# Seven-product form for four step pairs of a gate or feed-forward panel, a six-slot ring in the feed-forward block too, and two more gate panels a layer

## What is computed

```python
h = rms_norm(x, norm_g)
u = h @ w_in                      # 2048 -> 15944 columns, 8192 of them gates
...
for n, (y, z) in enumerate(((y_a, a_z), (y_b, b_z), (y_c, c_z), (y_m, m_z))):
    branch = y.reshape(B, S, W).astype(dt) * jax.nn.silu(z)
    merged = merged + jax.nn.sigmoid(gate_all[:, :, n]) * (branch @ w_branch[n])
return x + merged @ w_out
```

```python
gt, up = jnp.split(rms_norm_2(x, g_ffn) @ w_gate_up, 2, axis=-1)
return x + (jax.nn.silu(gt) * up) @ w_down
```

## Time and profile before

| | |
|---|---|
| median of the runs | 3272.08 us |
| the profiled execution's own time | 3272.8 us |
| its span, first to last instruction | 3271.0 us |
| PE busy | 3258.1 us |
| DVE busy | 2203.4 us |
| ACT busy | 1638.9 us |
| POOL (GpSimd) busy | 321.3 us |
| read from HBM | 609.80 MB, 189 GB/s over the span |

### The profile page before, as it was taken

The page is one execution under the profiler, slowest core; times in us unless marked ns, Lnnn a source line. Parts: engine busy times, 40 slices in busy tenths (PEclk is TensorE's granted clock), DMA queues, the critical chain, the costliest instruction groups (busy, mean ns, idle before and its releaser), DMA issues.

```text
span 3271.0 us, 39924 instructions
## 1 busy us (share of the span) xinstructions
PE 3258.1 (100%) x15091; PEld 2699.7 (83%) x15091; DVE 2203.4 (67%) x2476; ACT 1638.9 (50%) x2085; POOL 321.3 (10%) x282
## 2 busy tenths in 40 slices
PE   8999999999999999999999999999999999999999
PEld 7888888888888888888888888888888888888887
DVE  5466655588865656555888655575555578888887
ACT  6444445455544444454555445455444455555554
POOL 0111241100000102411000011160000100000000
PEclk9999999999999999999999999999999999999999
DMA  8665565666666655556665675554565656556655
GB/s 300 191 185 166 165 177 162 188 206 193 217 193 205 182 167 166 173 164 186 202 211 183 208 226 170 172 179 144 193 192 183 186 187 204 187 194 204 194 193 180
DMA packets 303808, 619.77 MB, mean 189 GB/s; under 512 B 24961, under 2 KB 29441, under 8 KB 302465
## 3 DMA queue, kind: packets, MB, share of 16 engines
q1 hardware_dynamic: 303616, 617.22, 60.9%
HBM read 609.80 MB, written 7.34 MB: 189 GB/s over the span
## 4 chain that ended last, share of the span: by engine, by line
PE 100%; DMA 0%; DVE 0%; ACT 0%; SPq 0%; issue 0%
PE G L1127 69%; PE X L1048 6%; PE X L1046 6%; PE X L1047 6%; PE X L826 2%; PE G L1048 2%; PE G L1047 2%; PE G L1046 2%; PE X L942 1%; PE X L914 1%; PE G L1121 1%; PE X L969 0%; PE X L968 0%; PE X L935 0%; PE X L916 0%; PE X L889 0%
## 5 line engine op out<-in xcount | busy, mean ns | idle before, releaser
L1452 DVE TENSOR_TENSOR w_lo<-raw,w_hi 128x1024 fp32r<-128x1024 f32 (+1 forms) x1016 | 1236.9, 1223 | 942.2 <-ACT w_hi L1148 915.4
L1148 ACT ACTIVATE w_hi<-raw 128x1024 fp32r<-128x1024 f32 (+1 forms) x1016 | 1052.8, 1041 | 1265.3 <-PE G L1127 1129.0
L1127 PE MATMUL G<-w_hi,xh 128*128 128x512 f32 x1984 | 796.0, 401 | 0.0
L1127 PE MATMUL G<-w_hi,xl 128*128 128x512 f32 x1984 | 775.0, 391 | 0.0
L1127 PE MATMUL G<-w_lo,xh 128*128 128x512 f32 x1984 | 772.7, 389 | 0.0
L1127 PE MATMUL G<-w_hi,yh 128*128 128x512 f32 x1256 | 499.3, 398 | 8.5 <-DVE w_lo L1452 8.5
L1127 PE MATMUL G<-w_hi,yl 128*128 128x512 f32 x1256 | 491.2, 391 | 0.0
L1127 PE MATMUL G<-w_lo,yh 128*128 128x512 f32 x1256 | 490.0, 390 | 0.0
L1127 PEld LDWEIGHTS G<-w_hi,xl 128*128 128x128 f32 x1984 | 372.3, 188 | 81.0
L1127 PEld LDWEIGHTS G<-w_hi,xh 128*128 128x128 f32 x1984 | 372.9, 188 | 73.9 <-issue 2.7
L1127 PEld LDWEIGHTS G<-w_lo,xh 128*128 128x128 f32 x1984 | 373.3, 188 | 72.2
(11 more groups left out here) (261 smaller groups left out, 3164.3 us busy)
## 6 DMA issues: line engine op xcount, KB each, us to landing
raw<-in_w_in SPq DMA_DIRECT2D x572, 512.0 KB, 3.6
raw<-in_w_gate_up SPq DMA_DIRECT2D x176, 512.0 KB, 4.1
raw<-in_w_down SPq DMA_DIRECT2D x88, 512.0 KB, 4.5
raw<-in_w_out SPq DMA_DIRECT2D x64, 512.0 KB, 4.2
raw_more<-in_w_in SPq DMA_DIRECT2D x52, 512.0 KB, 4.4
raw<-in_w_branch SPq DMA_DIRECT2D x48, 512.0 KB, 3.8
raw<-in_w_mem_kv SPq DMA_DIRECT2D x32, 512.0 KB, 6.3
raw<-in_w_o SPq DMA_DIRECT2D x32, 512.0 KB, 3.6
```

The lines of the kernel that those rows point to most:

```text
L1127: mm = M.matmul(G[blk.g][:, t, :], a[:, blk.kk + k, tok], ringed(w, blk, c)[:, j, :], start=(k == 0 and q == 0), stop=(k == blk.kt - 1 and ...
L1148: A(high_of(c)[:, 0:size_of(c)], source_of(c), ACT.Copy).then_inc(hi_done, 1)
L1452: V.tensor_tensor(low_of(c)[:, 0:n], source_of(c), high_of(c)[:, 0:n].bitcast(F32), ALU.subtract).then_inc(lo_done, 1)
```

## The change

Four edits, all in tables:

- `SEVENS` replaces `SEVEN`: the steps 1, 2, 4 and 5 take the seven-product form instead of 1, 3 and 5. One panel a layer, branch b's second, is `LIGHT` and keeps three (1, 2, 4).
- The gate blocks 0 and 1 of branch c become a panel, so a layer has six.
- `wide` now holds for every panel, and for the `down` blocks from the second group on: they use six slots. The first such use in the feed-forward block waits for the end of the last attention heads.
- The heads of m and b come four units apart instead of five: m from r+120, b from r+140; the forms, now four, at r+145, 149, 153, 157. The first panel begins at r+162. In the feed-forward block the fourth form is hung 18 units behind the first.

```diff
-SEVEN = (1, 3, 5)
+SEVENS = {0: (1, 2, 4, 5), 1: (1, 2, 4, 5), FF: (1, 2, 4, 5)}
+LIGHT = {("panel", l, "b", 1): (1, 2, 4) for l in range(DEPTH)}
+FORMS = max(len(s) for s in SEVENS.values())
...
+        self.seven = LIGHT.get(name, SEVENS[name[1]]) if kind == "panel" else ()
...
-                if br in WIDE_BRANCHES and (br, n // 2) != ("c", 0):
+                if br in WIDE_BRANCHES:
...
-        b.wide = (b.kind == "panel" and b.name[1] != FF) or (b.name[0] == "merge" and b.name[1] < DEPTH and ("panel", *b.name[1:3], b.name[3] // 2) in panels)
+        b.wide = b.kind == "panel" or (b.name[0] == "down" and b.name[1] > 0) or (b.name[0] == "merge" and b.name[1] < DEPTH and ("panel", *b.name[1:3], b.name[3] // 2) in panels)
...
-            soft(r + 121 + 5 * h, "m", l, h)
+            soft(r + 120 + 4 * h, "m", l, h)
         for h in range(H):
-            c = r + 146 + 5 * h
+            c = r + 140 + 4 * h
             at(c, "b_turn", l, h)
...
-        for i in range(len(SEVEN)):
-            at(r + 150 + 6 * i, "forms", l, i)
+        for i in range(len(SEVENS[l])):
+            at(r + 145 + 4 * i, "forms", l, i)
...
-    for i in range(len(SEVEN)):
+    for i in range(len(SEVENS[FF])):
         at(end_of("up", 0) + 4 + 6 * i, "forms", FF, i)
...
-                for l in range(DEPTH):
+                for l in PANEL_EVENTS:
                     if c in EXT_FIRST[l]:
-                        act.wait_ge(y_ready, Y_OF["norm", "b", l, H - 1] + 1)
-                        act.wait_ge(o_squared, NORM_OF["norm", "b", l, H - 1] + 1)
+                        if l == FF:
+                            act.wait_ge(y_ready, Y_OF["s_pv", "l", 2, HEADS2 - 1] + 1)
+                            act.wait_ge(x_sq_done, 16)
+                        else:
+                            act.wait_ge(y_ready, Y_OF["norm", "b", l, H - 1] + 1)
+                            act.wait_ge(o_squared, NORM_OF["norm", "b", l, H - 1] + 1)
```

More of the change, by code:

```diff
@@ L68, in chunks @@
     def chunks(self):
-        return sum(4 if s in SEVEN else 2 for s in range(STEPS)) if self.kind == "panel" else self.kt // self.ck
+        return sum(4 if s in self.seven else 2 for s in range(STEPS)) if self.kind == "panel" else self.kt // self.ck
     @property
@@ L162, in in_units @@
             loads += [(b, 2 * s), (b, 2 * s + 1)]
-            if s in SEVEN:
+            if s in blk.seven:
                 units += [(b, "low", s, k0 + 1), (b, "first", s, k0), (b, "sums13", s, None), (b, "sums24", s, None)]
@@ L179 @@
 LAST_PANEL = {l: max(b for b in PANELS if BLOCKS[b].name[1] == l) for l in PANEL_EVENTS}
-FORMS_DONE = {l: len(SEVEN) * (i + 1) for i, l in enumerate(PANEL_EVENTS)}
+FORMS_DONE = {l: sum(len(SEVENS[m]) for m in PANEL_EVENTS[:i + 1]) for i, l in enumerate(PANEL_EVENTS)}
 FF_PANEL = {b: i for i, b in enumerate(b for b in PANELS if BLOCKS[b].name[1] == FF)}
-STEM_ENDS = {SUMS_UNIT[b, SEVEN[-1]]: b for b in PANELS}
+STEM_END = {b: SUMS_UNIT[b, BLOCKS[b].seven[-1]] for b in PANELS}
+STEM_ENDS = {c: b for b, c in STEM_END.items()}
 def in_slots(wide, width):
@@ L212 @@
 BEHIND = {c: range(max(R_BEHIND[c], 0), R_BEHIND[c + 1]) for c in range(N_CHUNKS)}
-EXT_FIRST = {l: [min(c for c in range(FIRST_WIDE[l], N_CHUNKS) if U_SLOT[c] == k) for k in (4, 5)] for l in range(DEPTH)}
-EXT_LOAD = {l: min(r for r, (b, _s) in enumerate(LOADS) if b >= FIRST_PANEL[l] and R_SLOT[r] >= RING) for l in range(DEPTH)}
+EXT_FIRST = {l: [min(c for c in range(FIRST_WIDE[l], N_CHUNKS) if U_SLOT[c] == k) for k in (4, 5)] for l in PANEL_EVENTS}
+EXT_LOAD = {l: min(r for r, (b, _s) in enumerate(LOADS) if b >= FIRST_PANEL[l] and R_SLOT[r] >= RING) for l in PANEL_EVENTS}
 BLOCK = {b.name: i for i, b in enumerate(BLOCKS)}
@@ L552, in hybrid_program @@
         sums = over("sums", "arena", 0, [P, 2, 4, NB], F32)
-        form_hi_in = over("form_hi_in", "arena", 8192, [P, len(SEVEN), 4, P], F32R)
-        form_hi_ff = over("form_hi_ff", "arena", 4096, [P, len(SEVEN), 4, P], F32R)
+        form_hi_in = over("form_hi_in", "arena", 8192, [P, FORMS, 4, P], F32R)
+        form_hi_ff = over("form_hi_ff", "arena", 4096, [P, FORMS, 4, P], F32R)
         form_hi = {0: form_hi_in, 1: form_hi_in, FF: form_hi_ff}
-        form_lo = over("form_lo", "tmp", 0, [P, len(SEVEN), 4, P], F32R)
+        form_lo = over("form_lo", "tmp", 0, [P, FORMS, 4, P], F32R)
         form = [tmp[:, 3072 + 512 * i:3584 + 512 * i].rearrange("p (f t) -> p f t", t=P) for i in range(2)]
@@ L743, in back @@
             def back(l):
-                sp.wait_ge(lo_done, SUMS_UNIT[LAST_PANEL[l], SEVEN[-1]] + 1)
+                sp.wait_ge(lo_done, STEM_END[LAST_PANEL[l]] + 1)
                 if l:
@@ L1053, in by_form @@
             def by_form(l, s, f):
-                i = SEVEN.index(s)
+                i = SEVENS[l].index(s)
                 return form_hi[l][:, i, f, :], form_lo[:, i, f, :]
@@ L1073, in panel @@
                     _b, what, s, _r = UNITS[c]
-                    first, last = s == SEVEN[0], s == SEVEN[-1]
+                    first, last = s == blk.seven[0], s == blk.seven[-1]
                     pe.wait_ge(lo_done, c + 1)
@@ L1151, in stem @@
                 _, l, br, m = BLOCKS[b].name
-                act.wait_ge(mm_done, SUMS_UNIT[b, SEVEN[-1]] + 1)
+                act.wait_ge(mm_done, STEM_END[b] + 1)
                 if b == FIRST_PANEL[l]:
@@ L1852, in x_forms @@
             def x_forms(l, i):
-                k, n = 2 * SEVEN[i], FORM_N["forms", l, i]
+                k, n = 2 * SEVENS[l][i], FORM_N["forms", l, i]
                 if n >= 2:
@@ L1907, in _ @@
                 for i in range(H):
-                    if i < len(SEVEN):
+                    if i < len(SEVENS[l]):
                         x_forms(l, i)
```

## The result

The kernel takes 3286.87 us (median, 3286.63 to 3286.96) beside 3272.05 us for the kernel before on the same chip: a ratio of 1.0044, 95% interval [1.0033, 1.0056]. It is **slower by 14.8 us**; the forecast was 3261.8 us, and its range ended at 3269. None of the rivals describes what happened. (The title counts two more gate panels a layer; it is one more, made of two gate blocks, so six where there were five. And it leaves out the edit that decided the result, the heads four units apart.)

A forecast was written before the change was run, and what follows sets the result against it. PE's own work, busy 100% of the span, was taken as the bound. From the profiled 3272.8: - 14.8 + 3.8 - 1.0 + 0.4 + 1.2 = 3262.4, less 0.7 (profiled run over median), about 3261.8 us; range 3256 to 3269.

The forecast's parts named there:

- Heads closer together: Heads of m and b: stages share units oftener, PE breaks off 26 times less; -1.0 us, ends 0 and -2.3.
- the norm of m's queries: Heads of m: the norm ends on POOL 1.3 us before the first head's turn, so it costs nothing.
- b's tail: Ahead of the first panel: b's last head needs 2.97 us through DVE, PE gives about 2.9; +0.2 us a layer.
- 25 seven-product steps: Panels of both layers and feed-forward block: each added step saves 0.58 to 0.60 us of PE, 14.8 us in all.
- six slots: Feed-forward panels and downs, c's new panels: borrowed slots lengthen PE's work; +3.8 us, ends 0 and 6.
- fourth form: First feed-forward panel: PE waits for the form's low part, behind that panel's split on DVE; +1.2 us, once.
- tails: b's last head ahead of the first panel, both layers together: +0.4 us.
- DVE in double steps: Side-by-side seven-product steps: DVE falls back 3.3 us a pair but keeps 1.5 us margin in layer 0; no wait.
- Only the matmuls count: Rival: borrowed slots cost nothing in the feed-forward block, saved breaks count fully; 3256.7 us, chance 0.12.
- A thin hand-over opens: Rival: the feed-forward hidden block's low part comes 0.3 to 1 us late at eight panels; 3264 to 3270 us, chance 0.17.
- DVE paces the pairs: Rival: DVE operations don't overlap in double steps, PE waits some 1 us at 21 panels; 3283 us, chance 0.08.

The follow-up runs named there:

- experiment 2: Kernel before with only the heads of m four units apart instead of five: 3294.51 us, ratio 1.0066.
- experiment 4: Changed kernel, order untouched, but PE's logits of m's heads 1 to 3 wait for ACT's exponential instead of DVE's reciprocal: 3261.29 us, ratio 0.9966.
- experiment 7: Version of experiment 1 with three seven-product steps (1, 3, 5) in every panel, the light b panels too: 3276.75 us, ratio 1.0013.
- experiment 8: Kernel before with only the feed-forward block's panels and downs turned over six ring slots, three steps a panel: 3276.21 us, ratio 1.0011.
- experiment 3: Kernel before with only the heads of b four units apart instead of five: 3271.54 us, ratio 0.9998.
- experiment 11: Version of experiment 4 with the four forms of the feed-forward block five units apart instead of six: 3260.45 us, ratio 0.9962.
- experiment 6: Changed kernel with m's heads five units apart again, first at unit 119, b's first at 141: 3285.53 us, ratio 1.0038.
- experiment 9: Version of experiment 1 with the feed-forward block back on four ring slots, four steps a panel: 3283.99 us, ratio 1.0034.
- experiment 1: Changed kernel with the logits of m's heads a unit later, three units behind the head's start instead of two: 3264.74 us, ratio 0.9976.
- experiment 12: Version of experiment 11 with four seven-product steps in b's light panels too: 3264.64 us, ratio 0.9975.

## Why the prediction was wrong, point by point

The step that failed is "Heads closer together", -1.0 us with ends 0 and -2.3, and in it the sentence on the chains that become tighter. It lists two, the norm of m's queries and b's tail. A third was missing: the bank of logits. Two heads four units apart put the logits of one into the unit of the turn of the other, and the code frees that bank for m and l by DVE's reciprocal. This could be read before: from the table of stages, c + 4 + 2 = c + 6, and from the releases of that bank. The branch with heads already four apart, d, copies its scores out and frees the bank at once; l has its logits a unit later. m has neither. The prediction did see that stages would share a unit oftener, and booked it as a gain, fewer breaks; it did not ask what such a pair passes between them. The term was not -1.0 but +22.1 for m alone (experiment 2), +25.6 in the changed kernel.

The rest stood in the main. With that wait taken out (experiment 4) the same change takes 3261.29 us, 0.5 from the forecast. That closeness is in part luck: the kernel before took 3273.0 us in those runs, so the gain is 11.7 us where 10.3 were forecast; and two terms were sized too small, one a gain and one a cost, and cancel in part. By term:

| term | forecast | measured |
|---|---|---|
| 25 seven-product steps | -14.8 | 19 of them 12.0 (experiment 7), 0.63 each, so about -15.8, an estimate |
| six slots | +3.8, of it 2.5 worked out for the feed-forward block | +3.8 by the medians, 3.3 by the spans, for that block alone (experiment 8); the new panels of c not measured apart |
| heads closer, m | in -1.0 | +22.1 alone (experiment 2) |
| heads closer, b | in -1.0 | -0.9, not told from 0 (experiment 3) |
| fourth form | +1.2 | a wait of 1.2; -0.8 when it goes (experiment 11) |
| tails | +0.4 | no wait; a unit later 11.1 (experiment 6) |
| DVE in double steps | 0 | 0 with six slots; +19.3 with four, feed-forward alone (experiment 9) |

The sum of the measured terms without m's, -15.8 + 3.8 - 0.9 + 1.2, gives -11.7 us, the same as experiment 4 against its own kernel before (3261.29 - 3273.0). It is less exact than it looks, since b's -0.9 is not told from nothing.

A feed-forward period shows the two sizes that were off: a fourth step gives 0.64 us (64.77 in experiment 7, 64.13 now) where 0.59 was taken, and six slots cost up to 0.39 where 0.28 was taken, so the 64.1 us foretold came true with both terms too small. Two slips in the working are without weight: the sum gives 3261.7, not 3261.8, and the tail's 2.97 us against 2.9 are 0.1 us a layer, not 0.2.

The rivals. "Only the matmuls count" fell with experiment 8. "A thin hand-over opens" did not happen: in the feed-forward block PE waits once, for the form. "DVE paces the pairs" did not either: DVE's 57.9 us a period are those of overlapping operations. With four slots PE does wait for DVE inside the pairs, but for want of room and not of DVE's speed: with six slots the same work brings no wait, and here DVE is busy in only 37.73 of a slow panel's 43.68 us:

```profile
2792.03:2835.71 43.68, 42.66 (x182) 33.33 (x181) 37.73 (x41) 24.72 (x28) 0.00 (x0) 1.00 0.56 185
```

The chance of 0.09 for "slower" was too low for another reason than any price: all of it hung on the panels, since the closer heads had been written off as work moved and not as waits.

## What to carry to other kernels

When stages move closer, list every buffer that passes from one to the next, and for each the operation that gives it back and what stands ahead of that operation on its engine. A release tied to an operation behind the last true reader costs nothing until the next user comes near, and then it costs a whole place in another engine's queue: here 25.6 us for reciprocals of 0.16 us each. And price a wait of TensorE at more than the profile records: part of it is hidden under the matmul before, and behind some of the longer ones the matmuls run at the lower clock.

## What the runs showed of the hardware

In the changed kernel four of six waits of 2.2 to 3.2 us of TensorE were followed by a stretch at the lower clock, as from 505.65 to 510.2 with starts 0.43 us apart; a wait of 3.00 us and one of 2.20 in layer 1 were not. In experiment 6 both waits of 5.5 us were. Behind waits of 1.6 us or less the clock stayed full (experiments 1, 9 and 12). The profile counts idle time from the recorded end of a matmul, 0.39 us behind its start, though the next could start after 0.23; late starts of 22.4 us show as some 8.6 us of waits (experiment 9). Six slots lengthen TensorE's work by 3.4 us in 2679 matmuls, by no more than 0.011 us at any one of them (experiment 8); why stays open, and no run tried it.
